# Seven pairs of input products as 2x2 block products ahead of the state-space branch, with their results kept in DRAM

## The reference, cut to what matters

```python
xn = rmsnorm(x, attn_norm_g)
proj = xn @ w_in                       # u_pool, q/k/v of the dilated attention, q/k/v of the
                                       # stick-breaking attention, u_s5
y_pool, y_dil, y_sb, y_s5 = four branches, each from its columns of proj
for bi, yb in enumerate((y_pool, y_dil, y_sb, y_s5)):
    gate = jax.nn.sigmoid(xn @ w_gate[bi])
    merged = merged + gate * (yb @ w_branch[bi])
x = x + merged @ w_out
```

## Time and profile before

| | us |
|---|---|
| median of 3 runs | 3352.51 (3352.19 to 3353.46) |
| the profiled execution, its own time | 3352.35 |
| its span, first to last instruction | 3350.6 |
| PE busy | 3274.1 |
| DVE busy | 1949.7 |
| ACT busy | 1312.7 |
| POOL busy | 470.7 |
| moved by DMA | 352.71 MB, mean 105 GB/s |

### The profile page before, as it was taken

How to read it: one execution, slowest core, us unless ns; L and a number is a source line. 1 busy time by engine, 2 the same in 40 slices (tenths; PEclk the granted TensorE clock), 3 DMA queues, 4 the chain that set the end, 5 groups by cost and what they waited for, 6 DMA issues and landing times.

```text
span 3350.6 us, 38566 instructions
## 1 busy us (share of the span) xinstructions
PE 3274.1 (98%) x15624; PEld 2670.1 (80%) x15624; DVE 1949.7 (58%) x2354; ACT 1312.7 (39%) x1882; POOL 470.7 (14%) x369
## 2 busy tenths in 40 slices
PE   8999999999999999999999999999989999999998
PEld 6888888877877778888888887777788778888886
DVE  8564462333655535677773265445476789888226
ACT  4342111444256623433331047354455554444213
POOL 0000000000000000454540010000020026554000
PEclk9999999999999999999999999999999999999999
DMA  3313242111510123223328422221204322334721
GB/s 125 78 57 125 99 156 78 45 51 61 195 50 26 36 78 126 95 107 113 113 106 317 149 88 100 75 101 38 103 5 164 120 84 107 112 114 165 301 99 51
DMA packets 115250, 352.71 MB, mean 105 GB/s; under 512 B 16104, under 2 KB 26088, under 8 KB 115056
## 3 DMA queue, kind: packets, MB, share of 16 engines
q1 hardware_dynamic: 112960, 349.91, 29.8%
q10 hardware_dynamic: 2112, 0.33, 0.1%
HBM read 265.53 MB, written 83.48 MB: 104 GB/s over the span
## 4 chain that ended last, share of the span: by engine, by line
PE 85%; DVE 7%; ACT 5%; issue 1%; DMA 1%; SPq 0%; ACTq 0%; DVEq 0%
PE PS L496 45%; PE PS L2479 22%; PE PS L479 8%; PE PS L1961 1%; PE PS L1939 1%; PE PS L514 1%; ACT whi L436 1%; PE PS L1631 1%; PE PS L3923 1%; DVE wlo L441 1%; ACT dS L1687 1%; DVE FT L3796 0%; PE PS L3934 0%; PE PS L1606 0%; DMA slot<-hid 0%
## 5 line engine op out<-in xcount | busy, mean ns | idle before, releaser
L441 DVE TENSOR_TENSOR wlo<-raw,whi 128x1024 fp32r<-128x1024 f32 (+3 forms) x380 | 480.8, 1265 | 391.4 <-ACT whi L436 388.8
L436 ACT CAST whi<-raw 128x1024 fp32r<-128x1024 f32 (+3 forms) x380 | 359.2, 945 | 686.8 <-PE PS L496 340.7
L496 PE MATMUL PS<-xhi,whi 128*128 128x512 f32 x1872 | 601.7, 403 | 6.7 <-DVE wlo L441 2.1
L496 PE MATMUL PS<-xlo,whi 128*128 128x512 f32 x1872 | 579.2, 391 | 0.0
L496 PE MATMUL PS<-xhi,wlo 128*128 128x512 f32 x1872 | 577.8, 390 | 0.0
L496 PEld LDWEIGHTS PS<-xhi,whi 128*128 128x128 f32 x1872 | 344.9, 188 | 91.6 <-issue 14.8
L496 PEld LDWEIGHTS PS<-xlo,whi 128*128 128x128 f32 x1872 | 352.0, 188 | 75.3
L496 PEld LDWEIGHTS PS<-xhi,wlo 128*128 128x128 f32 x1872 | 352.0, 188 | 75.3
L2479 PE MATMUL PS<-tf,whi 128*128 128x512 f32 x936 | 288.1, 389 | 0.0
L2479 PE MATMUL PS<-xhi,whi 128*128 128x512 f32 x624 | 242.8, 389 | 2.5 <-DVE xlo L2464 2.5
L2479 PE MATMUL PS<-xhi,wlo 128*128 128x512 f32 x624 | 242.7, 389 | 0.0
(11 more groups left out here) (601 smaller groups left out, 5468.0 us busy)
## 6 DMA issues: line engine op xcount, KB each, us to landing
raw<-in_w_up SPq DMA_DIRECT2D x88, 512.0 KB, 3.8
hid<-hs SPq DMA_DIRECT2D x88, 512.0 KB, 3.6
raw<-in_w_in SPq DMA_DIRECT2D x67, 512.0 KB, 3.5
slot<-hid SPq DMA_DIRECT2D x56, 512.0 KB, 6.9
adr<-in_w_ada SPq DMA_DIRECT2D x48, 512.0 KB, 4.5
raw<-in_w_down SPq DMA_DIRECT2D x40, 512.0 KB, 3.5
raw<-in_w_gate SPq DMA_DIRECT2D x32, 512.0 KB, 3.5
merged<-hid SPq DMA_DIRECT2D x16, 512.0 KB, 12.7
```

The costliest lines, as they stand in the source:

```text
L436: act.e.copy(whis[place(i)][:, ks, :], raws[i % RING][:, ks, :]).then_inc(*give("w_hi", i))
L441: dve.e.tensor_tensor(wlos[place(i)][:, ks, :], raws[i % RING][:, ks, :], whis[place(i)][:, ks, :].bitcast(F32), ALU.subtract).then_inc(*g ...
L496: ins = pe.e.matmul(ps[:, h * 512:(h + 1) * 512], w[s][:, k, :], x[:, h * 512:(h + 1) * 512], start=(at == 0 and n == 0), stop=(at == kt - ...
```

## The change

The following products leave their places: the gates 3 and 7 of branch 3, 3 and 7 of branch 0, 5 and 7 of branch 2, and w_in 4, 5, 16 to 21 (the first queries and all values of the dilated attention). They become seven pairs (`PASS`), computed as 2x2 blocks behind w_in 37 and ahead of the state-space work. Gate 3 of branch 1 leaves its merge too and joins `BESIDE`, which w_in 36 and 37 leave; these two are now plain products right behind w_in 35. `SLOTS` changes from 21, 3, 10 to 9, 5, 10 steps.

```diff
-EARLY_S5 = ((3, 2), (3, 4), (3, 6), (0, 0), (0, 2), (0, 4), (0, 6), (1, 0), (1, 6), (2, 6), (3, 0))
+EARLY_S5 = ((3, 2), (3, 4), (3, 6), (0, 0), (0, 2), (0, 4), (0, 6), (1, 0), (1, 6), (2, 6), (1, 3), (3, 0))
+PASS = ((("w_gate", 27), ("w_gate", 31)), (("w_gate", 3), ("w_gate", 7)), (("w_gate", 21), ("w_gate", 23)), (("w_in", 4), ("w_in", 5)),
+        (("w_in", 16), ("w_in", 17)), (("w_in", 18), ("w_in", 19)), (("w_in", 20), ("w_in", 21)))
...
-            next(powers, None)
             begin_dve(dve, "w_in", 34)
             begin_dve(dve, "w_in", 35)
-            s5_coefficients(dve)
+            pass_sum(dve, 2)
+            pass_sum(dve, 4)
+            pass_lo(dve, 3)
+            pass_lo(dve, 4)
+            begin_dve(dve, "w_in", 36)
+            begin_dve(dve, "w_in", 37)
+            pass_dve(dve, [powers, s5_coefficients(dve)])
...
-        SLOTS = [("cl", 21), ("k", 3), ("ks", 10)]
+        SLOTS = [("cl", 9), ("k", 5), ("ks", 10)]
```

```diff
+                part(a, 0, PX11, "p1", ("sv_p1", 0, p), "sv_1", 0, p)
+                part(a, 4, PX21, "p2", ("sv_c11", 0, p), "prod", a)
+                pe.wait_ge("t_lo", 0, 4)
+                part(b, 4, PTF[4], "p4", ("sv_c21", 0, p), "prod", b)
+                pe.wait_ge("t_lo", 0, 1)
+                part(s12, 0, PTF[1], "p5", ("sv_p5", 0, p), "sv_5", 0, p)
+                pe.wait_ge("t_lo", 0, 2)
+                part(s12, 4, PTF[2], "p6", ("sv_u2", 0, p), "prod", s12)
+                part(s34, 0, PTF[3], "p7", ("sv_u3", 0, p), "sv_7", 0, p)
+                part(s34, 4, PX22, "p3", ("sv_c12", 0, p), "prod", s34)
...
+                begin_dve(dve, *PASS[p][1])
+                if p:
+                    next(beside, None)
+                begin_dve(dve, "pass_s12", p)
...
+            sp.wait_ge("sv_5", 0, NPASS - 1)
+            for m in range(2):
+                sp.e.dma_start(PTF[1][m].bitcast(F32), BACKUP[m]).then_inc(*land("xn_back", m))
...
         def s5_pool(pool):
-            pool.wait_ge("xn_lo", 7, 1)
-            pool.wait_ge("bsc")
+            pass_pool(pool)
+            pass_cleared(pool, 0, 1, 2)
             pool.e.memset(Mk, 0.0).then_inc(*give("s5_mzero"))
```

All fourteen results go to DRAM (512 KB each). The gates come back in the merges in the way of the other early gates. Queries and values come back in the dilated attention; the values of group g+1 are loaded while group g runs:

```diff
+            def values(g):
+                for n in range(2):
+                    if g:
+                        sp.wait_ge("dil_vT", g - 1, n)
+                    sp.wait_ge(*stored(4 + g, n))
+                    sp.e.dma_start(Vf[:, n, :], spill[:, 6 + 2 * g + n, :]).then_inc(*land(f"lane{2 + n}", "dv", g))
...
-                for n, ring in enumerate((side_ring, o_ring)):
-                    product(pe, ring, "w_in", 16 + 2 * g + n, XN, ("dil_v", g, n))
                 turned(g, 0)
```

More of the change, by code:

```diff
@@ new lines, in build, with pass_slot, pass_turn, put_half @@
+        BACKUP = [spill[:, 2 * m:2 * m + 2, :].rearrange("p a (b c) -> p (a b) c", b=2) for m in range(2)]
+        def pass_slot(name, ft):
+            return 18 + ft if name == "w_gate" else {4: 4, 5: 5}.get(ft, ft - 10)
+        def pass_turn(name, ft):
+            return DILS[(ft - 16) // 2] if name == "w_in" and ft >= 16 else 1
+        def put_half(p, x, hf):
+            r = pass_turn(*PASS[p][x])
+            n = 512 // r
+            return PUT[2 * (p % 2) + x].rearrange("p (r l) -> p l r", r=r)[:, n * hf:n * hf + n, :]
@@ new lines, in build, with pass_pe, part @@
+        pass_ring = [6, 7, 4, 5, 0, 1, 2, 3]
+        def pass_pe(pe):
+            for n in range(8):
+                bank.read_by[n] = psum.read_by.get(n // 2, ())
+            ring = list(pass_ring)
+            for p in range(NPASS):
+                a, b = (pe.next_product(name, ft) for name, ft in PASS[p])
+                s12, s34 = pe.next_product("pass_s12", p), pe.next_product("pass_s34", p)
+                def part(unit, at, x, name, read, *signal):
+                    w, ps = unit % RING, bank.take(pe, ring, (name, 0, p), read)
+                    pe.wait_ge("w_lo", unit)
+                    for k in range(4):
+                        for n, (ws, xs) in enumerate(((whis, x[0]), (whis, x[1]), (wlos, x[0]))):
+                            ins = pe.e.matmul(ps, ws[w][:, at + k, :], xs[:, k, :], start=(k == 0 and n == 0), stop=(k == 3 and n == 2))
+                    ins.then_inc(*give(*signal))
+                part(a, 0, PX11, "p1", ("sv_p1", 0, p), "sv_1", 0, p)
[8 more added lines that the diff above has]
+                part(s34, 4, PX22, "p3", ("sv_c12", 0, p), "prod", s34)
+            for n in range(4):
+                psum.read_by[n] = bank.read_by[2 * n] + bank.read_by[2 * n + 1]
@@ L863, in stream @@
                 for p, (name, ft) in enumerate(BESIDE):
-                    done = ("s5_u", ft - 34) if name == "w_in" else ("gate", ft // 8, ft % 8)
-                    yield from product_steps(pe, [0, 1] if p % 2 == 0 else [1, 0], name, ft, XN, done)
+                    order = (4, 5, 6, 7, 0, 1, 2, 3) if p == 0 else None
+                    yield from product_steps(pe, [0, 1] if p % 2 == 0 else [1, 0], name, ft, XN, ("gate", ft // 8, ft % 8), order=order)
             steps = stream()
@@ L899, in beside_sp @@
                     begin_sp(sp, name, ft)
[L900 removed]
+                elif p < len(BESIDE) - 1:
                     sp.wait_ge("gate", ft // 8, ft % 8)
@@ L909, in s5_sp @@
             begin_sp(sp, "w_in", 35)
+            sp.wait_ge("xn_lo", 3, 1)
+            for m in range(2):
+                sp.e.dma_start(BACKUP[m], PTF[1][m].bitcast(F32)).then_inc(*land("xn_saved", m))
+            begin_sp(sp, "w_in", 36)
+            begin_sp(sp, "w_in", 37)
+            pass_sp(sp)
             beside_sp(sp, "cl")
@@ L928, in s5_pe @@
             rows_ring = [2, 3]
+            for n in range(2):
+                product(pe, [n], "w_in", 36 + n, XN0, ("s5_u", 2 + n))
+            pass_pe(pe)
             beside = beside_pe(pe)
@@ L1579, in dil_sp @@
                         next(side, None)
+                    if i == 3 and g < 2:
+                        values(g + 1)
                     if i >= 3:
@@ L1701, in dil_act @@
             for g in range(3):
[L1702 to L1705, removed]
+                for n in range(2):
+                    i = begin_act(act, "w_in", 10 + 2 * g + n)
                     act.wait_ge("prod", i)
```

229 lines of the change are left out of this document (194 added, 35 removed).

## The result

| | us |
|---|---|
| before, median of 12 runs | 3352.35 (3350.75 to 3358.09) |
| changed kernel, median of 12 runs | 3359.52 (3355.97 to 3362.14) |
| ratio, changed to before | 1.0019, 95% interval 1.0011 to 1.0027 |
| changed kernel, profiled execution | 3358.0, span 3356.2 |

The change took out 20 us of matmuls and made the kernel about 7 us slower. The first row of the page shows the trap: PE is busy 9.7 us less than in the earlier trace rows, with 84 fewer matmuls, and the span is longer all the same.

A forecast was written before the change was run, and what follows sets the result against it. The prediction took PE, busy 98% of the span, as the bound: the number of matmuls and PE's standing still. Nine terms sum to +5.0 on 3352.35, giving 3357.4 us, range 3346 to 3368.

The forecast's parts named there:

- 2: Front: DVE's sums cause no stall, waits of 1.2 and 1.5 us go, save and reload cost nothing: -2.7 us.
- 4: Merge 3: PE stands still 4.0 us at the first tiny matmuls for the eighth ada, second half slips 0.5: +4.5 us.
- 9: Clock: PE loses 1.7 us at the lower level for each of three new idle times in the merges: +5.1 us.
- 1: Products: fourteen separate products computed as seven pairs in 2x2 passes: -19.6 us.
- 3: Passes: the small DVE chain now runs inside them, nearly hidden: +0.5 us.
- rival C: Passes stall as chain pieces or strided results hold the weights, up to 4 us in each of two: 3365 us, chance 0.08.
- 5: Merge 0: PE stands still 5.7 us at the first tiny matmuls, second half 0.5: +6.2 us.
- 6: Merge 1: without gate 3 ahead, PE stands still 7.7 us at the tiny matmuls for the eighth ada: +7.6 us.
- 7: Merge 2: branch 5 waits 2.1 us for weights, where 0.9 was waited: +1.4 us.
- 8: Dilated attention: the strided key copy is less covered ahead of the scores, twice 1.0 us: +2.0 us.
- A: Whole kernel: ada and its loads run further ahead, so fewer matmuls make it faster: 3344.5 us, chance 0.14.
- B: Merges 3 and 0: loads become the bound, +7 us and a further fall of the clock: 3366 us, chance 0.3.

The follow-up runs named there:

- e4: Changed kernel with two transfers issued earlier by SP (the reload of xn, the copies of Ks to Mk): 3359.38 us, ratio 1.0020.
- e3: Changed kernel with gate 3 of branch 1 put back into merge 1, in place of the state-space branch: 3358.52 us, ratio 1.0019.
- e5: Changed kernel with one side-product step moved ahead of the first scores in each group of the dilated branch: 3359.43 us, ratio 1.0025.
- e8: Kernel before with only gate 3 of branch 1 moved from merge 1 to beside the state-space branch: 3360.77 us, ratio 1.0028.
- e9: Changed kernel with the first tiny matmuls of three merges issued one branch product later: 3348.93 us, ratio 0.9992.
- e1: Changed kernel with the first tiny matmuls of three merges, and their mod addition, issued two branch products later: 3343.82 us, ratio 0.9972.
- e6: Changed kernel with useless matmuls in the idle time ahead of the first tiny matmuls of merges 0 and 1: 3353.85 us, ratio 1.0005.
- e7: Changed kernel with the edits of e1, e4 and e5 together: 3338.29 us, ratio 0.9960.

## Why the prediction was nearly right, and where its steps were not

The forecast was 3357.4, +5.0; the profiled execution came out at 3358.0 and the median at 3359.5. That the sum fits so well is luck: between the table's columns the stages are off by 16 us in size (merge 3 alone by 6.5), with signs that leave +0.6. What was right is the mechanism, small dependent steps that lose the product ahead of them; terms 2, 4 and 9 had wrong steps.

**1 and 3, and rival C.** As foretold, and C did not come. The passes are one stretch of 133.5 us for 588 matmuls, from 71.54 on (72.2 foretold), with the small chain inside; its +0.5 was not there.

**2, the front, failed by 2.6 us with 3.** The reload "has about 13 us" of cover, I wrote, counted from the part that frees its place. But it stands in SP's queue behind a raw load, and that load waits for a weight part that DVE ends at 202.8; the reload was issued at 203.17 (197.00 in e4) and PE waited 2.3 us for it. The instructions queued ahead of the moved one had been counted, but not what they wait for. The other part is the wait for `work`, 2.1 before and 3.8 now, behind the queue of SP shown in section 6.

**4, merge 3, failed: 0.8 us idle where 4.0 stood.** The step was "0.52 MB in about 1.9 us", from the mean of a 9 us window. The mean of a window in which the queue also pauses is not the rate at which a waiting load comes in. The first row is from the kernel before, the others from the changed kernel:

```profile
451.60:455.00 3.40, 3.40 (x17) 2.81 (x16) 1.39 (x2) 0.62 (x1) 0.00 (x0) 1.00 1.00 367
455.00:458.40 3.40, 3.40 (x16) 2.82 (x15) 2.48 (x3) 1.05 (x1) 0.00 (x0) 1.00 0.99 381
458.40:461.80 3.40, 3.40 (x16) 2.82 (x15) 2.45 (x2) 0.62 (x1) 0.00 (x0) 1.00 1.02 394
```

So 285 was not the busiest that the old trace had; 367 was there to be read, and its page has a slice of 84 us at 317. At 390 GB/s 0.52 MB takes 1.35 us, and DVE waited 1.06 and 0.64 for loads here, where it had waited 3.48 in the earlier trace rows. The Trainium skill, DMA: Bandwidth & Descriptors, Specifications, gives 358 GB/s for one core; as an upper limit these windows don't bear it out, but it was nearer than the 285 that I took. The Trainium skill, HBM Reference, Specifications (TRN2), adds that a core streaming alone measures well above that share, about 425 GB/s; with 394 the trace agrees. With no wait in the second half, where 0.5 stood, and no fall of the clock behind so short a wait in this trace, merge 3 cost 0.8 us.

**5, merge 0.** 3.5 us idle for 5.7 in this trace, but 4.5, 5.4 and 5.2 in those of e3, e4 and e5, so the idle time was oversized by less than one trace says; its third of the clock term was undersized, 3.4 for 1.7.

**6, merge 1, was right** at 7.8 idle for 7.7, because it came from DVE's own rows and from no rate of a transfer. Runs e8 and e9 bear out its rule, the lateness of ada less the PE work ahead of it.

**7 and 8.** Merge 2 waited 2.5 us for weights (2.1 foretold) and cost 0.9. The keys cost 2.6 us of waits where 2.0 stood, and the stage has one short stretch at half clock more than before (two for one, 1.7 us each); together with small differences it came to 3.6.

**9, the clock, failed in its size.** "3 x 1.7" took the price behind one wait of 2.1 us for all lengths. The traces give (us; lost is half of PE's work in the stretch):

| wait | idle | at half clock | of it PE works | lost |
|---|---|---|---|---|
| before, `work` | 2.1 | 3.4 | 3.4 | 1.7 |
| changed, `work` | 3.8 | 3.5 | 3.5 | 1.7 |
| changed, merge 0 | 3.5 | 6.8 | 6.8 | 3.4 |
| e9, merge 1 | 5.0 | 10.3 | 8.2 | 4.1 |
| e5, merge 0 | 5.2 | 10.3 | 9.2 | 4.6 |
| e1, `work` | 5.5 | 6.9 | 6.1 | 3.0 |
| changed, merge 1 | 7.8 | 13.7 | 7.9 | 4.0 |

```profile
259.40:262.90 3.50, 3.50 (x14) 2.81 (x12) 0.00 (x0) 1.01 (x1) 0.00 (x0) 0.51 0.07 26
907.90:913.70 5.80, 0.04 (x1) 0.04 (x1) 5.57 (x6) 0.00 (x0) 0.00 (x0) 0.51 0.97 324
913.70:921.60 7.90, 7.90 (x27) 6.93 (x28) 1.47 (x3) 0.00 (x0) 0.00 (x0) 0.50 0.50 180
```

These rows are the changed kernel's. The loss behind one wait is 1.7 to 4.6 us and does not follow from its length alone: 3.8 us were followed by half of what 3.5 were, and behind 7.8 us much of the stretch ran while PE still stood. Nothing follows merge 3's 0.8 us in the changed kernel's trace; in e6's, 3.4 us at half clock begin 3 us behind the same wait. Between 30 and 1400 us the changed kernel has 30.7 us at half clock, the kernel before 6.8.

**The rivals.** A (the matmul count decides) fell by its own sign, idle time at L1514, and e1 shows how near it was: with that idle time away the kernel is at 0.9972. B (the loads become the bound) fell too: DVE's waits for adr sum to 7.7 us over three merges (11.1 in the kernel before), 1.6 the longest, and the DMA engines moved 346 GB/s in the first half of merge 3, where B wanted less than 250.

So the 19.6 us went, and 5.6 more, in the profiled pair: 11.8 in merge 1, 7.0 in merge 0, 3.6 in the dilated attention, 2.8 elsewhere. The first two are shown by experiment: of their 18.8 us 15.7 came back with e1, its control at nothing. The 3.6 are argued from waits, since e5 won nothing back. The 1.8 us behind 1400 us were not tried; the changed kernel's trace has one 3.4 us stretch at half clock more there, which alone is 1.7.

## What to carry to other kernels

Before a product is taken from in front of a small dependent step, ask how late that step's input is: the product was its cover. Here 12 us of waits at a few tiny matmuls, and the 7 that the clock took behind them, undid 20 us of saved matmuls, and issuing them two products later won back 16 without changing any work. The same question has to be put at the other end, where a product is taken away again (e3), and to the queue of a moved transfer, with all that the instructions ahead of it wait for.

## What the runs showed that I had not expected

- Issuing DMAs from two queues at once made ACT's issues slower: four copies on its queue took 9.95 us beside SP's (9.97 in e7) and 4.14 without. SP's four took 6.95 us beside ACT's and 6.84 without.
- An idle time of PE costs more than its length: 3.4 and 4.0 us lost to the clock behind 3.5 and 7.8 us, and useless matmuls in those gaps won back 4.7 us of the total.
- The DMA engines moved 394 GB/s over 3.4 us in merge 3, beside PE at full clock, where I had read 285 as the most.
- Where nothing was edited, traces still differ in their waits and half-clock stretches: the wait in merge 0 was 3.5 us in one and 5.2 in another, with 6.8 and 10.3 us at half clock behind it. Twelve runs of the changed kernel spread over 6.2 us, so a difference of 1 to 3 us between two single profiles needs a second look.
